# Where the modulation chunks stand in the gate stage of layer 0: behind the next gate's weight split, or ahead of it

## What is computed

```python
mod = jax.nn.silu(cond) @ lp['w_ada'] + lp['b_ada']            # 6 * 1024 values per group
sh1, sc1, g1, sh2, sc2, g2 = jnp.split(mod[:, None, :], 6, axis=-1)
h = x * (1.0 + sc1) + sh1
q, k, v, z_hy, gate_a, gate_b = jnp.split(h @ lp['w_in'], SPLITS, axis=-1)
# attn: windowed attention of q, k, v;  hy: Hyena long convolution of z_hy
merged = (jax.nn.sigmoid(gate_a) * (attn @ lp['w_pa'])
          + jax.nn.sigmoid(gate_b) * (hy @ lp['w_pb']))
x = layer_norm(ALPHA * x + g1 * (merged @ lp['w_out']), ...)
x = layer_norm(ALPHA * x + g2 * conv_ffn(x * (1.0 + sc2) + sh2), ...)
```

## Time and profile before

| | |
|---|---|
| median of 3 runs | 2243.01 us (2241.37 to 2246.72) |
| profiled execution, time | 2241.82 us |
| profiled execution, span | 2240.0 us |
| granted TensorE clock, mean | 0.966 |
| busy, share of span | PE 93%, weight loads 88%, DVE 52%, ACT 34%, POOL 7% |

### The profile page before, as it was taken

One profiled execution on the slowest core, in us unless ns is written; L12 is line 12 of the kernel. 1 busy time (PEld: TensorE's weight loads), 2 busy tenths in 40 slices (PEclk: granted clock), 3 DMA queues, 4 the chain that ended last, 5 costly groups with the idle time before them and its releaser, 6 DMA issues.

```text
span 2240.0 us, 30937 instructions
## 1 busy us (share of the span) xinstructions
PE 2075.8 (93%) x13302; PEld 1976.1 (88%) x13302; DVE 1170.1 (52%) x1716; ACT 757.0 (34%) x1114; POOL 167.6 (7%) x183
## 2 busy tenths in 40 slices
PE   7899978788889999999999999799999999999997
PEld 5888857788888999999998888579999999999996
DVE  3354577644447677777544454774235533234335
ACT  1534444311116331233234443452223533123323
POOL 0300000100015000000022000010002300000011
PEclk9989999999999999999999999899999999999998
DMA  6311121233321334444322101112121211222121
GB/s 243 110 54 39 36 84 49 94 113 105 112 95 57 132 145 159 177 151 151 116 78 76 67 22 58 63 49 84 66 97 48 88 66 56 82 95 76 58 66 48
DMA packets 32721, 199.37 MB, mean 89 GB/s; under 512 B 3926, under 2 KB 4487, under 8 KB 14280
## 3 DMA queue, kind: packets, MB, share of 16 engines
q1 hardware_dynamic: 30424, 188.23, 23.7%
q0 software_dynamic: 2160, 9.16, 1.2%
HBM read 194.49 MB, written 2.88 MB: 88 GB/s over the span
## 4 chain that ended last, share of the span: by engine, by line
PE 80%; DVE 9%; ACT 5%; issue 4%; DMA 1%; POOL 1%; SPq 0%; DVEq 0%; ACTq 0%; POOLq 0%
PE gemm_psum L515 46%; PE gemm_psum L545 14%; PE gemm_psum L565 3%; PE gemm_psum L583 3%; PE aux_psum L630 2%; PE gemm_psum L528 2%; PE aux_psum L682 2%; DVE aux_psum L1302 2%; PE aux_psum L615 2%; PE aux_psum L670 2%; ACT w_hi L919 1%; PE gemm_psum L670 1%; DVE w_lo L1314 1%; PE aux_psum L639 1%; PE gemm_psum L462 1%
## 5 line engine op out<-in xcount | busy, mean ns | idle before, releaser
L515 PE MATMUL gemm_psum<-h_hi,w_hi 128*128 128x322 f32 x2176 | 511.2, 316 | 44.9 <-DVE gates L1638 39.3
L515 PE MATMUL gemm_psum<-h_hi,w_lo 128*128 128x322 f32 x2176 | 506.9, 315 | 0.0
L515 PE MATMUL gemm_psum<-h_lo,w_hi 128*128 128x322 f32 x2176 | 505.8, 314 | 0.0
L1314 DVE TENSOR_TENSOR w_lo<-w_raw,w_hi 128x2048 fp32r<-128x2048 f32 (+3 forms) x146 | 292.3, 2002 | 352.1 <-ACT w_hi L919 350.4
L515 PEld LDWEIGHTS gemm_psum<-h_hi,w_hi 128*128 128x128 f32 x2176 | 374.0, 193 | 52.1 <-issue 51.8
L515 PEld LDWEIGHTS gemm_psum<-h_lo,w_hi 128*128 128x128 f32 x2176 | 373.8, 192 | 0.0
L515 PEld LDWEIGHTS gemm_psum<-h_hi,w_lo 128*128 128x128 f32 x2176 | 373.6, 192 | 0.0
L919 ACT ACTIVATE w_hi<-w_raw 128x2048 fp32r<-128x2048 f32 (+3 forms) x146 | 243.4, 1667 | 159.3 <-PE gemm_psum L545 65.6
L1302 DVE CUSTOM_DVE_ANT_0 aux_psum<-w_raw,cond_by_row 128x1024 f32<-128x1024 f32 x160 | 191.0, 1256 | 3.9 <-DMA w_raw<-in_ada_t 3.7
L1431 DVE SCALAR_TENSOR_TENSOR x<-gemm_psum,mod,x 128x128 f32<-128x128 f32 (+2 forms) x144 | 55.3, 434 | 167.7 <-PE gemm_psum L545 131.6
L545 PE MATMUL gemm_psum<-act_hi,w_lo 128*128 128x322 f32 x616 | 141.9, 311 | 0.0
(11 more groups left out here) (298 smaller groups left out, 3264.1 us busy)
## 6 DMA issues: line engine op xcount, KB each, us to landing
w_raw<-in_w_up SPq DMA_DIRECT2D x44, 1024.0 KB, 4.9
w_raw<-in_ada_t SPq DMA_DIRECT2D x40, 1024.0 KB, 4.7
w_raw<-in_w_down SPq DMA_DIRECT2D x32, 704.0 KB, 4.2
w_raw<-in_w_gate SPq DMA_DIRECT2D x16, 1024.0 KB, 4.8
w_raw<-in_w_z SPq DMA_DIRECT2D x12, 1024.0 KB, 4.7
w_raw<-in_ada SPq DMA_DIRECT2D x8, 1024.0 KB, 6.1
w_raw<-in_w_proj SPq DMA_DIRECT2D x16, 512.0 KB, 3.5
w_raw<-in_w_out SPq DMA_DIRECT2D x8, 1024.0 KB, 4.7
```

The lines of the kernel that those rows point to most:

```text
L515: last = mm(gp[:, 2 * (t % 2) + hf, 0:HALF], w[:, off + P * kk:off + P * (kk + 1)], moving(kk, lo)[:, hf * HALF:(hf + 1) * HALF], start=kk ...
L1314: TT(wlo[s][:, 0:n], raw[STEP[(lane.layer, "g", g)] % 2][:, 0:n], f32(whi[s][:, 0:n]), ALU.subtract).then_inc(sem["w_split"], raised("w_sp ...
```

## The change

In DVE's order of a gate tile the chunks move ahead of the split of gate m + 1, between the two splits. The slots are keyed by the gate GEMM in place of the projection GEMM, so in the stream the chunks stand behind projection m and ahead of gate m + 1, where they stood behind gate m + 1 and ahead of projection m + 1. The number of chunks at each tile and their order stay. In the memory layout `kcT` and `k_out` move from the region that later holds the Hyena rows into the one of `k` and `v_tok`, which grows by 16 floats, and a placeholder in the feed-forward region goes away.

```diff
@@ -91,7 +91,7 @@
 for _m in range(KD):
     _n = 1 + _m % 2
-    ADA_SLOTS[at_g("proj", _m)], _due = _due[:_n], _due[_n:]
+    ADA_SLOTS[at_g("gate", _m)], _due = _due[:_n], _due[_n:]
...
-KV_SPACE = 3 * HY_W
+KV_SPACE = 3 * HY_W + 16
...
             k = sb("k", [P, 1, ROW], F32, s2)
             vtok = sb("v_tok", [P, NB, P], F32, s2)
+            kcT = sb("kcT", [P, P], F32, s2)
+            kout = sb("k_out", [P, P], F32, s2)
...
             osb = sb("o_sb", [P, 4 * P], F32, s2)
-            kcT = sb("kcT", [P, P], F32, s2)
-            kout = sb("k_out", [P, P], F32, s2)
...
-        with ExitStack() as s2:
-            sb("cond_space", [P, 2, D_MODEL], F32, s2)
...
                 g = at_g("gate", m)
                 if m:
                     split(g + 1)
-                split(g + 2)
                 if L == 0:
                     if m == 0:
                         dve.wait_ge(sem["cond_rows"], 1)
-                    for to, c in ADA_SLOTS[g + 1]:
+                    for to, c in ADA_SLOTS[g]:
                         ada_t(to, c)
+                split(g + 2)
                 for c in range(2):
                     dve.wait_ge(sem["gate_out"], due("gate_out", 2 * m + c + 1))
```

## The result

The changed kernel takes 2186.12 us (median; 2182.64 to 2192.11) against 2242.36 us of the kernel before in the same comparison: ratio 0.9748, 95% interval 0.9723 to 0.9773. The forecast was 2186.2 us, in a range of 2179 to 2197.

A forecast was written before the change was run, and what follows sets the result against it. PE waiting for DVE's product in layer 0's gate stage was taken as the bound. The 63.06 us difference to layer 1's stage, less 4.04 and 2.2 us for tile 0, gave 56.8 us gain: 2186.2 us, range 2179 to 2197.

The forecast's parts named there:

- What bounds, and the floor: PE waits for DVE's product in layer 0's gate stage; layer 1's stage, without chunks, is its measured floor.
- Chunks under gate m: Chunks fit into DVE's 12.10 us idle before the gate split, leaving 2.5 us with two, 7.4 us with one.
- The stream: SP's two raw slots: gate weights load behind the chunks, landing 0.5 us before ACT needs them on two-chunk tiles.
- the prediction's own signs of being wrong: PE waiting for w_lo or DVE for w_raw over about 2 us on odd tiles, tile 0's wait vanishing, clock near 0.91.
- 6.75 us to land in: Time a gate weight load may take on two-chunk tiles before PE idles: 4.8 + 0.5 + 1.4 us.
- DVE's 3.9 us: How late DVE can be on a two-chunk tile before PE feels it, some 3.9 us.
- Tile 0: Its chunk has no gate stage to hide in; 3.97 us of the 4.61 us PE wait stay.
- slow start: PE's first 20 matmuls behind tile 0's wait take 5.26 us against 3.05 at full clock, 2.2 us lost.
- The layout: Moving kcT and k_out costs nothing, the split taking 2.29 us from either raw slot; 1 us either way in the range.
- The clock time was given back: 15.6 us of slow clock in layer 0's gate stage goes with the idle; the opposing rival gave 2199.6 us, chance 0.05.
- rival 2 and 3: Late gate loads: landings at some 10.7 us give 2211 us, chance 0.05; at 21 us, 2252 us, slower, chance 0.03.
- Rival 4: Chunks still run after w_hi because their load comes late, so PE waits as now: 2243 us, chance 0.03.

The follow-up runs named there:

- The order alone: The changed order of DVE and of the weight stream on the old memory layout, against the kernel before: 2184.23 us, ratio 0.973.
- the layout alone: Only the memory layout of the change, with the old stream and DVE order, against the kernel before: 2243.69 us against 2242.54, ratio 1.0003.
- the products ahead of the chunks: New layout, old stream order, DVE's chunks moved behind their tile's products and lo part, against the kernel before: 2190.32 us, ratio 0.9772.
- the filled kernel: Kernel before with chunk reductions writing to one place and extra PE matmuls during waits: 2241.54 us, ratio 0.9999; without those matmuls 2257.26 us.

## Why the prediction was right

**The number and the mechanism.** The mechanism is borne out: seven waits became one, of the size and at the place forecast, and the stage lost 57.6 us where 56.8 were forecast. That the medians agree to 0.1 us (2186.12 and 2186.2) is luck: the four executions spread over 9.5 us, and the profiled one, put at 2185.0 us, took 2192.11.

**What bounds, and the floor.** Right. Layer 1's stage was taken as the floor for layer 0's, and tile 0 free of its chunk reached it: 189.31 us against 189.21.

**Chunks under gate m.** Right, and close: 2.5 us of DVE's idle was to be left on two-chunk tiles (2.47 measured in tile 3) and 7.4 on one-chunk tiles (7.16 to 7.36). In tile 1 it is 4.53 us, mainly because gate 1 starts slowly and so ends later. That reductions beside gate matmuls cost nothing was argued from reductions beside projection matmuls; the 189.31 us with tile 0 free show it.

**The stream.** Right for two chunks: no PE wait. But one of the prediction's own signs of being wrong was met: DVE was to wait for w_raw by no more than about 2 us on odd tiles, and in tile 7 it waited 2.42 us. The prediction had priced a late gate load, with 6.75 us to land in; the second chunk's load, which it had landing just as the first chunk ended, has no time of its own in hand, only DVE's 3.9 us. In tile 7 it landed 7.1 us after its issue in place of 4.8, and those 3.9 us covered it. The order alone shows the same in tile 7, with 6.4 us to landing and a wait of 1.7 us; the kernel with tile 0 free doesn't. Why this load is late is open. With three chunks the chain of the loads was worked out and met, 2.54 to 3.04 us for 2.7.

The two places that draw on the Trainium skill now read as follows. From the Trainium skill, DMA: Bandwidth & Descriptors (Bandwidth, "Measured"; Anatomy of one DMA), the prediction made an estimate of 8.15 us for a 1 MB load, by which 1.4 us of PE idle were to come on each two-chunk tile. There is none, for the page of the profile after has 4.7 us for the landing of the gate's loads (KB each, us to landing):

```profile
w_raw<-in_w_gate SPq DMA_DIRECT2D x16, 1024.0 KB, 4.7
```

The 8.15 us added two figures that don't belong to one sum: under Anatomy of one DMA that page of the Trainium skill puts a load at about 2.0 us plus its bytes at 436 GB/s, which for 1 MB is an estimate of 4.4 us, and the trace's 4.7 us is near that.

The Trainium skill, TensorE: Matmul & The Clock Gate (What's actually happening), says not to rely on an exact number of slow matmuls, and the traces agree: behind tile 0's wait, 3.88 us in the changed kernel and 3.87 us in the order alone, six pairs start slowly in the one and ten in the other.

**Tile 0.** Right: 3.97 us forecast, 3.88 measured, start of gate 1 at 26.80 us into the stage forecast and 419.78 - 393.06 = 26.72 measured. Its slow start was put at 2.2 us. The stage is 194.70 - 189.21 = 5.5 us over the floor, 4.0 us of it the later start, so 1.5 us were slow clock. In the order alone, with the same wait, the same sum leaves 2.6 us of the stage's 195.71. So the forecast's 2.2 us, read behind one wait of 4.61 us, lies between two measurements that differ by 1 us for the same wait, and being off by 0.7 us here means little. The stage's gain is 57.6 us in the one and 56.6 in the other, for 56.8.

**The layout.** Costs nothing beyond the interval of the layout alone. Rows 4 and 6, which the prediction reads for it, don't name the raw slot of a split, so they don't show the same time from either.

**The rivals.** The clock time was given back: the stage's granted clock went from 0.91 to 0.99. Loads as late as rival 2 and 3 need didn't occur; their mechanism is real, as three chunks show, but needed half as much work again in a tile. Rival 4 fell with the order of DVE's rows.

**What the profiled span seems to deny.** It fell by 49.7 us, not 57.6. The difference lies outside the stage: its first matmul is at 393.06 against 388.57, after instructions that the change doesn't touch, and 3.4 us more come behind it. The same 56 us of each kernel ahead of the stage, in the kernel after:

```profile
168.00:224.00 56.00, 53.03 (x348) 49.27 (x346) 21.45 (x41) 17.72 (x35) 0.00 (x0) 0.86 0.11 39
```

And in the kernel before:

```profile
168.00:224.00 56.00, 53.03 (x394) 49.14 (x394) 23.57 (x44) 22.54 (x46) 0.00 (x0) 1.00 0.11 39
```

At 0.86 of the clock against 1.00, PE gets through 348 matmuls against 394. How much of this the other executions have, no profile shows.

## What to carry to other kernels

When an engine works through a list in order, look at what stands between a wait that it must make and the result that another engine is held up by, and move independent work to the far side of that wait; the idle time ahead of the wait, read from a sister stage without that work, says how much fits. A ring of load slots is moved along with the order by the rule of its slots (the products ahead of the chunks did with the old one, at a small price), and its chain (this load is issued when the chunk before is used up) can end later than the engine's own work, as three chunks on a tile did. The first turn of a pipeline has no earlier stage to hide work in: it is worth giving it none, which brought another 5 to 6 us in the stage here.

## What the runs showed of the hardware

Short waits can cost clock as well. With two matmuls to a pair, waits of 1.19 to 1.39 us left the pairs behind them 0.30 us apart; waits of 2.54 to 3.04 us with three chunks on a tile were followed by pairs 0.54 us apart (0.68 of the clock in the 5.27 us behind one of them) and cost 1.5 us each on top of the idle. How much a wait costs isn't fixed by its length: waits of 3.88 and 3.87 us cost 1.5 and 2.6 us, and in the filled kernel a wait of 2.92 us was followed by pairs at 0.30 us and one of 3.02 us by pairs at 0.54. Keeping PE busy with matmuls whose result nobody reads brought the granted clock of the stage from 0.89 to 0.99 and its length down by 9.9 us.

The time up to the gate stage, with the same instructions in all of these kernels, ran from 381.6 us (old order, filled) to 393.06 us (changed kernel). That is more than twice the 0.2% that a comparison of medians tells, so a difference of single spans says little; the length of the stage in question says much more.
